# Three stacked transformer blocks on one core: 16 gate projections moved from fp32 weights to split halves kept in DRAM, with another order of work in the recurrent heads and at stage ends

## What is computed

```python
def first_block(x, ...):            # layer 0: pool_mixer, layer 1: dilated attention with 3 groups
    h = layer_norm(DN_ALPHA * h + pool_mixer(h, ...), ...)
    kv = h @ w_kv
    h = layer_norm(DN_ALPHA * h + dilated_mixer(h, w_in_b, w_out_b, k_sh, v_sh, slopes), ...)

def second_block(x, ...):           # hybrid layer: short convolution, sparse attention, gated MLP
    ...

def third_block(x, ...):            # one layer
    h = rmsnorm_3(x, norm1_w) * (1 + sc1) + sh1
    pq, pff, pfb, pi, pg, pa, pb, pgh, pgc = split_proj(h @ w_in)   # pff, pfb: the two gates
    k, log_g = hgrn2_gates(pff or pfb, lb)        # k = sigmoid(-f), log_g = log(clip(sigmoid(f)))
    o_lat = hgrn2_bidir(pq, pi, pff, pfb, ..., s_f, s_b)            # 8 heads of 128 channels
    x = x + gt1 * mixer_merge(o_lat, pg, pa, pb, pgh, pgc, ...)
    x = x + gt2 * conv_ffn(rmsnorm_3(x, norm2_w) * (1 + sc2) + sh2, ...)
    return rmsnorm_3(x, final_norm_w)
```

## Time and profile before

| what | value |
|---|---|
| time, median of 3 runs | 3195.84 us (3194.66 to 3197.61) |
| profiled execution: its own time | 3202.15 us |
| its span | 3200.4 us |
| mean granted TensorE clock | 0.988 |
| TensorE busy | 3098.9 us, 97% |
| VectorE, ScalarE, GpSimd busy | 1568.5, 1051.3, 1575.8 us |
| HBM read, written | 309.90 MB, 22.54 MB |

### The profile page before, as it was taken

One profiled execution on the slowest core, in us unless ns is written; L12 is line 12 of the kernel. 1 busy time (PEld: TensorE's weight loads), 2 busy tenths in 40 slices (PEclk: granted clock), 3 DMA queues, 4 the chain that ended last, 5 costly groups with the idle time before them and its releaser, 6 DMA issues. The chain is left out here.

```text
span 3200.4 us, 46074 instructions
## 1 busy us (share of the span) xinstructions
PE 3098.9 (97%) x17626; PEld 2412.3 (75%) x17626; DVE 1568.5 (49%) x2637; ACT 1051.3 (33%) x2171; POOL 1575.8 (49%) x891
## 2 busy tenths in 40 slices
PE   8999999999999999999999999998888999999998
PEld 7887897777775877777778777775555886878886
DVE  4771202333343155445421354737777897667731
ACT  2110312333324244444421223637776202221111
POOL 6665565443433444344477765710002564656664
PEclk9999999999999999999999999999999999999999
DMA  4222322323235222222355452322221221222221
GB/s 166 96 99 99 123 94 80 115 97 113 100 113 195 79 103 80 96 103 80 103 184 217 170 173 92 111 86 76 71 80 67 86 92 66 98 75 98 99 96 56
DMA packets 97708, 338.04 MB, mean 106 GB/s; under 512 B 10737, under 2 KB 12913, under 8 KB 97362
## 3 DMA queue, kind: packets, MB, share of 16 engines
q1 hardware_dynamic: 89568, 319.63, 28.5%
q10 hardware_dynamic: 7234, 12.98, 1.2%
q0 software_dynamic: 688, 2.49, 0.3%
HBM read 309.90 MB, written 22.54 MB: 104 GB/s over the span
## 5 line engine op out<-in xcount | busy, mean ns | idle before, releaser
L300 PE MATMUL psum<-arena_r,ring_r 128*128 128x512 f32 (+1 forms) x3216 | 1248.7, 388 | 0.0
L298 PE MATMUL psum<-arena_r,arena_r 128*128 128x512 f32 (+1 forms) x3096 | 1220.7, 394 | 26.2 <-DVE arena_r L610 8.4
L288 POOL TENSOR_SCALAR arena_r<-ring 128x1024 fp32r<-128x1024 f32 x431 | 461.6, 1071 | 1516.4 <-PE psum L300 1011.2
L299 PE MATMUL psum<-arena_r,arena_r 128*128 128x512 f32 (+1 forms) x3096 | 1197.3, 387 | 0.0
L290 POOL TENSOR_TENSOR ring_r<-ring,arena_r 128x1024 fp32r<-128x1024 f32 x431 | 1061.9, 2464 | 75.5 <-issue 43.1
L298 PEld LDWEIGHTS psum<-arena_r,arena_r 128*128 128x128 f32 x3096 | 584.6, 189 | 161.9 <-issue 33.5
L300 PEld LDWEIGHTS psum<-arena_r,ring_r 128*128 128x128 f32 x3216 | 609.5, 190 | 124.9
L299 PEld LDWEIGHTS psum<-arena_r,arena_r 128*128 128x128 f32 x3096 | 585.0, 189 | 117.2 <-issue 4.1
L935 DVE SCALAR_TENSOR_TENSOR arena<-arena,con,psum 128x256 f32<-128x256 f32 x64 | 30.8, 481 | 388.5 <-PE psum L859 388.5
L2900 DVE SCALAR_TENSOR_TENSOR psum<-arena,par,psum 128x512 f32<-128x512 f32 x215 | 152.0, 752 | 8.9
L1492 DVE SCALAR_TENSOR_TENSOR arena<-arena,con,psum 128x128 f32<-128x128 f32 (+1 forms) x64 | 35.1, 548 | 227.0 <-PE psum L1342 227.0
(11 more groups left out here) (420 smaller groups left out, 4017.6 us busy)
## 6 DMA issues: line engine op xcount, KB each, us to landing
ring<-in_weights SPq DMA_DIRECT2D x535, 512.0 KB, 3.3
ring_r<-half_store SPq DMA_DIRECT2D x32, 512.0 KB, 3.3
half_store<-arena_r SPq DMA_DIRECT2D x16, 512.0 KB, 4.8
half_store<-ring_r SPq DMA_DIRECT2D x16, 512.0 KB, 5.5
gate_store<-arena ACTq DMA_DIRECT2D x14, 256.0 KB, 3.8
arena<-in_x_t SPq DMA_DIRECT2D x8, 256.0 KB, 4.9
arena<-arena ACTq DMA_DIRECT2D x16, 128.0 KB, 3.4
arena<-gate_store ACTq DMA_DIRECT2D x1, 2048.0 KB, 10.8
```

What stands on the lines that cost most here:

```text
L288: nc.gpsimd.tensor_scalar(hi_part(t), src, 1.0, 1.0, ALU.mult, ALU.mult)
L298: nc.tensor.matmul(out, w_hi, a_hi, start=start, stop=False)
L299: nc.tensor.matmul(out, w_hi, a_lo, start=False, stop=False)
L300: return nc.tensor.matmul(out, w_lo, a_hi, start=False, stop=stop)
```

## The change

1. Sixteen tiles with the gate weights f and b of the heads are loaded and split in the first attention, among the tiles of the next pair's projections: before fillers 3 and 6 of each of seven groups, and before filler 1 of groups 2 and 4 (`first_keeps`). ScalarE makes the high half three fillers ahead, after an evacuation, GpSimd the low half, SP stores both. `half_store` has 32 entries. In the heads all four parts are now 12 products on halves, and a head takes 8 ring tiles from DRAM instead of 6.
2. In the heads TensorE's `outputs` come after the first projection half; on ScalarE `copy_far` and `keys(hd, 1)` come first in step 6; on VectorE `diagonal` moves from step 6 to step 5 ahead of `sums`, and the second direction of `states` from step 7 to step 0 of the next head, behind `fill`.
3. At the start TensorE runs three products on ones, tile 0 is split in two pieces (a quarter first), and its first blocks need only the first piece.
4. `residual_norm`: VectorE multiplies by the scale too, ScalarE only adds the shift.
5. In both last norms the sum of squares is added before the next product is awaited, and `tiles_together` comes ahead of the taking of banks 6 and 7.

```diff
+def first_keeps():
+    return sorted([7 * g + i for g in range(KT - 1) for i in (3, 6)] + [7 * g + 1 for g in (2, 4)])
...
-                hd, r = divmod(t - heads_at[0], 6) if heads_at else (-1, 0)
-                if 0 <= hd < KT and r >= 2:
-                    sp.dma_start(lo_part(t).bitcast(F32), half_store[2 * hd + r // 2 - 1, r % 2]
+                hd, r = divmod(t - heads_at[0], 8) if heads_at else (-1, 0)
+                if 0 <= hd < KT:
+                    sp.dma_start(lo_part(t).bitcast(F32), half_store[4 * hd + r // 2, r % 2]
...
                 for k in range(KT):
-                    nc.vector.tensor_tensor(z[:, k], z[:, k], psum[:, 5], ALU.mult).then_inc(scaled_k, 1)
+                    nc.vector.scalar_tensor_tensor(z[:, k], z[:, k], scale_of(k), psum[:, 5], ALU.mult,
+                                                   ALU.mult).then_inc(scaled_k, 1)
...
-                    nc.scalar.activation(h[:, k], z[:, k], ACT.Identity, scale=scale_of(k), bias=bias_of(k))
+                    nc.scalar.activation(h[:, k], z[:, k], ACT.Identity, bias=bias_of(k))
...
+            keep_hi = [as_r(74, 2)]
...
+                for i in range(3):
+                    nc.tensor.matmul(psum[:, 0], ubuf_ones[:, 0:P], ubuf_ones, start=True, stop=True)
+                bank_take(pe, 0)
+                for k in range(KT):
+                    pe.wait_ge(x_lo_in, k + 1)
+                    if k == 0:
+                        pe.wait_ge(first_part, 1)
+                    elif k == 2:
+                        pe.wait_ge(w_split, split_no[0] + 1)
+                    last = three(psum[:, 0], w_hi[:, k], w_lo[:, k], x_hi[k], x_lo[k], k == 0, k == KT - 1)
...
-                load_tiles(sp, Q0 + RING, O0 + EARLY - Q0)
+                t = Q0 + RING
+                for j in range(KEPT_FIRST):
+                    load_tiles(sp, t, keep_at(j) + 6 - t)
+                    t = keep_at(j) + 6
+                    keep_store(sp, keep_at(j), j, keep_hi, keep_lo_in, kept_in, 4 * (j // 2) + j % 2)
+                load_tiles(sp, t, O0 + EARLY + RING - t)
...
                     if filler(n) is not None:
-                        tile_columns(pe, q_at(*filler(n)), 1, h_hi, h_lo)
+                        f = 7 * p + n % UN
+                        kept = (kept_in, 32 * (keeps.index(f) + 1)) if f in keeps else None
+                        tile_columns(pe, q_at(*filler(n)), 1, h_hi, h_lo, kept=kept)
...
                     if filler(n) is not None:
                         evacuate(act, *filler(n))
+                        f = 7 * p + n % UN + 3
+                        if f in keeps:
+                            j = keeps.index(f)
+                            keep_high(act, keep_at(j), j, keep_hi, keep_hi_in, kept_in)
...
-                        if n_t == 2:
-                            w_hi, w_lo = (lo_part(u).rearrange("p (b m) -> p b m", m=P) for u in (t, t + 1))
-                            last = three(psum[:, b], w_hi[:, k], w_lo[:, k], n_hi[k], n_lo[k], k == 0, k == KT - 1)
-                        else:
-                            last = nc.tensor.matmul(psum[:, b], slot(t % RING)[:, k], hn[:, k], start=(k == 0),
-                                                    stop=(k == KT - 1))
+                        w_hi, w_lo = (lo_part(u).rearrange("p (b m) -> p b m", m=P) for u in (t, t + 1))
+                        last = three(psum[:, b], w_hi[:, k], w_lo[:, k], n_hi[k], n_lo[k], k == 0, k == KT - 1)
...
                         scores(NS * hd + i)
-                        if i == 0 and hd:
-                            outputs(pe, hd - 1)
...
                             tail_half(i // 2, i % 2)
+                        if i == 0 and hd:
+                            outputs(pe, hd - 1)
...
+                        if i in (6, 7):
+                            copy_far(s - 1)
+                        if i == 6:
+                            keys(hd, 1)
                         if i + 2 < NS - 1:
                             level_exp(s + 2)
...
-                        if i in (5, 6):
-                            keys(hd, i - 5)
-                        if i in (6, 7):
-                            copy_far(s - 1)
+                        if i == 5:
+                            keys(hd, 0)
...
-                        elif i == NS - 2:
-                            diagonal(s + 1)
+                        if i == 0 and hd:
+                            states(hd - 1, 1)
...
                         if i == NS - 3:
                             fill(s + 1)
+                            diagonal(s + 2)
...
                         if i == 7:
                             states(hd, 0)
-                            states(hd, 1)
+                            if hd == KT - 1:
+                                states(hd, 1)
...
                 for m in range(KT):
+                    if m >= 2:
+                        dve.wait_ge(sq_done, m)
+                        nc.vector.tensor_tensor(st2[:, 1], st2[:, 1], sq2[:, (m - 1) % 2], ALU.add)
+                        dve.drain().then_inc(sq_added, 1)
                     dve.wait_ge(w_used, O0 + m + 1)
...
+                tiles_together(pe, [(U0, 0), (U0 + 1, 3)], h_hi, h_lo, h_lo_in)
                 bank_take(pe, 6)
                 bank_take(pe, 7)
-                tiles_together(pe, [(U0, 0), (U0 + 1, 3)], h_hi, h_lo, h_lo_in)
```

102 lines of the change are left out of this document (67 added, 35 removed).

## The result

The kernel after takes 3158.41 us (median of 4 runs, 3156.05 to 3162.85), the kernel before 3195.51 (3194.66 to 3197.61, 4 runs): a ratio of 0.9886, with a 95% interval of 0.9873 to 0.9898. Forecast were 3159.0 us and a range of 3140 to 3178, so the total is right to 0.6 us. That this is so close is partly luck: the parts miss by up to 4 us each and make up for one another. The experiments show that the size of the heads' gain was right in all and two of its causes were not, and that the kept tiles cost nothing that can be seen.

A forecast was written before the change was run, and what follows sets the result against it. The heads were taken as bound by a chain over VectorE and ScalarE. Terms -31 + 3 - 1.1 - 0.9 - 6.2 - 0.6 = -36.8 us, against the median 3195.84, gave 3159.0 us; range 3140 to 3178.

The forecast's parts named there:

- Bound of the heads: the chain over VectorE and ScalarE: Heads, gates to gates: a chain over VectorE and ScalarE sets the loop, which goes from 41.4 to 37.2 us.
- With TensorE 0.68 us quicker a level these 2.1 us close.: Heads: faster half projections close ScalarE's waits of 0.79 and 1.28 us between level 2's exp and gates.
- Together 3.5 us ... 1.4 given back: Heads, VectorE: diagonal and second states leave the path, 3.5 us; states ahead of level 2's diff cost 1.4.
- Head 0: First head: 2.7 us gained by faster projections ahead of the loop, 0.7 by its loop.
- All heads: Recurrent heads: -31 us in all, 25.2 of it from six loops; ends -20 and -55.
- The square: Heads, ScalarE: outputs come at most 3 us later, about when ScalarE reaches their square; counted as nothing.
- rival (a): Heads: ScalarE waits for the outputs, roots and gates slide; heads gain only 20 us, 3170 in all; chance 0.22.
- Kept tiles, +3: First attention: 16 kept tiles mostly hidden, two closer ones cost 1.5 us each; bounds nothing and 56 us.
- Rival (d): First attention: the one high buffer makes ScalarE stand in keep_high; slower than before from 24 us on; chance 0.07.
- rival (c): First attention: GpSimd's subtractions hold VectorE; if all 39 us reach TensorE, 3195, no change; chance 0.05.
- Before the feed-forward, -6.2: Last norm into feed-forward: tiles_together no longer behind bank 7, so the 49th product comes 6.2 us sooner; ends -4 and -7.
- Rival (b): Heads: TensorE becomes the bound and all of the three passes pays; heads -55 us, 3135 in all; chance 0.11.

The follow-up runs named there:

- e2: Kernel before with only the new order of the three engines in the heads, fp32 gate projections and no kept tiles: 3171.69 us, ratio 0.9922.
- e1: Kernel after with the order of all three engines in the heads as before, gate projections still in three passes: 3176.56 us, ratio 0.9940.
- e6: Kernel after with TensorE's outputs of the last head back ahead of the first projection half: 3165.95 us, ratio 0.9901.
- e12: Kernel after with only ScalarE's new order kept in the heads, TensorE's outputs and VectorE's diagonal and second states back as before: 3167.50 us, ratio 0.9906.
- e7: Kernel after with VectorE's second states back at level 7, ahead of the next head's first level: 3159.51 us, ratio 0.9882.
- e8: Kernel after with ScalarE's copy_far and second-direction keys back behind the next head's first exp, VectorE's and TensorE's order new: 3183.09 us, ratio 0.9956.
- e9: Kernel after with the second states moved behind level 2's diff on VectorE and the outputs' square behind ScalarE's next exp: 3152.41 us, ratio 0.9861.
- e4: Kernel after without GpSimd's subtraction for the 16 kept tiles, the raw tile stored for the low half: 3161.34 us, ratio 0.9886.
- e5: Kernel after with neither ScalarE's copy nor GpSimd's subtraction for the kept tiles, the slot stored twice: 3159.07 us, ratio 0.9880.
- e3: Kernel after with start, norm scale, both sums of squares and tiles_together's place as before, heads and kept tiles staying: 3167.24 us, ratio 0.9906.

## Why the prediction was right, and where it was not

- *Bound of the heads: the chain over VectorE and ScalarE.* Right. At the full clock e2, whose TensorE has 2.7 us more of products in each loop, has the same loop as after. But its TensorE is then busy 36.27 of 36.72 us, so it shows no more than that the chain is the longer of two nearly equal bounds there. Forecast were 37.2 us a loop, measured 37.5.
- *"With TensorE 0.68 us quicker a level these 2.1 us close."* The waits closed, the cause is another. The step that failed is the one that gave the three passes 2.1 us a loop: alone they give 1.0 (41.1 to 40.1, e1), and under the new order 0.1 on the mean. The waits are closed in e2 as well, with fp32 products, and still there, shorter, in e1, e6 and e12 with three passes. What closes them is the outputs' new place on TensorE (e6), for which the prediction counted nothing.
- *"Together 3.5 us ... 1.4 given back"*, the diagonal and the second states leaving VectorE's path. Too much for the states: e7 shows them worth 0.6 to 0.7 us a loop, not 1.5, and 1.1 in the time. Their wait for chunk sums goes through ScalarE's move alone (e12). The diagonal's 0.6 was not tested by itself. What was given no price of its own, `copy_far` and `keys` ahead of the exp, is worth 24.7 us with the other moves there (e8) and 9.1 without them (e12). I had called TensorE "lying partly beside" the chain and booked its 4.15 us nowhere. They were in it: over the five loops VectorE stands 26.6 us for scores and 9.0 for chunk sums in before, 15.3 and 11.2 in e1, 5.5 and nothing in after.
- *Head 0.* Forecast 2.7 for the passes and 0.7 for the order, measured 47.4 - 44.0 = 3.4, all of it by the passes (e2 has 47.4). *All heads:* from the first gates to the last scores 356.7 us before and 325.3 after, 31.4 less; forecast 31. Here is the luck: the six ways between the second and the last gates give 18.3 + 3.4 = 21.7, forecast 25.2, and behind the last gates 6.4 come, forecast 2.1. What the last head gained beyond its 2.1 was not looked into.
- *The square.* "ScalarE reaches it at about that moment": it reaches it 0.85 us early, so rival (a) is true in its mechanism and small in its size. That the wait counts is seen in after's own first loop, which has neither the wait nor the stretch at the low clock ahead of it and takes 36.7 us against 37.6 to 37.8, and with e9, where it goes together with the 1.4 us of the states and the loop loses 1.5.
- *Kept tiles, +3.* Nothing that can be seen: 425.1 us against 425.0, and e4 and e5 find nothing to give back. Rival (d) is out by the ScalarE rows (no wait for stores), rival (c) by e4: VectorE passes are stretched, by what is open, but into its slack.
- *Start, -1.1:* -0.87. *Before the feed-forward, -6.2:* from the first low half (2817.35 before, 2777.5 after) to the 49th product it took 18.0 us and takes 11.9, so -6.1. *Norm scale, -0.6:* the bias-only pass of that norm lasts 0.707 us, 0.80 before, eight of them 0.7.
All the small terms together were 8.8 us in the sum and 8.8 in e3 by the medians, 6.4 by the ratios.

- *Rival (b), TensorE the bound:* not in after, nor in e9; in e2 it is near.

The profiled executions are 3202.15 and 3156.05 us, 46.1 apart where the medians are 37.1 apart: the one lies 6.3 us above its median, the other 2.4 below. Some 4 us of it lie in the first attention (429.2 and 425.1 us), where the change has no part in it (e2, with before's code there, has 425.0). The sum without the +3 would have been -39.8, and the medians show -37.1: the +3 that did not come is what makes the match so close. So the forecast was rightly made as a difference and set against the median.

## What to carry to other kernels

A wait of the busiest engine that seems to lie beside the chain should be followed forward before it is priced at nothing: here it fed the very waits that were booked under other names, and one move of two ScalarE operations was worth more than all the faster products. Moves of an order are not additive; price each by what it would be worth with the others in place, and test it by taking it alone out of the finished kernel. Work for a side engine costs nothing where the main engine is the bound and its neighbours have slack, and costs most of the time by which it holds up a neighbour on the chain (here 5.2 of 8.1 us): so it belongs in the attention, not in the heads. And before two kernels' loops are compared by their means, look at the granted clock of each loop.
